# The begin of the MLPs, reordered: fewer parts between the rounds, six products of the second pair in front, modulation one unit on

## Chip, cores and metric

The kernel runs on one core of one Trainium2 chip. The metric is device time in microseconds of one launch. A core has TensorE (PE, matrix products into eight PSUM banks of 128 x 512 fp32), VectorE (DVE), ScalarE (ACT), GpSimd (POOL) and SyncE (SP), which issues nearly all DMAs here. Each engine works through its own instructions in order and waits on semaphores of the others.

## The reference, cut to what matters

Two residual blocks with an MLP each (layers 0 and 1), then a third block with an adaptive modulation. What the change touches:

```python
for l in range(2):
    ...
    mo = memory_attention(mq, mk, mv)                       # layer 0: "m0"
    x = x + jnp.concatenate([mixed, mo], axis=-1) @ w_out[l]
    x = x + jnp.square(jax.nn.relu(rms_norm(x, mlp_norm[l]) @ w_up[l])) @ w_down[l]
...
mod = jax.nn.silu(c) @ w_ada + b_ada                        # 1024 -> 3072, for the third block
```

Sequence 1024, width 1024, MLP width 4096, all fp32.

## The kernel before, in words

**Numbers.** Every fp32 operand of a large product is split into a high part (ACT, a rounding copy to fp32r) and a low part (DVE, the rest), and a product is three matmuls: high x high, high x low, low x high.

**The memory stage of layer 0** (`pe_mem0`, `act_mem0`, `dve_mem0`, `sp_x0`) runs in ten units. PE weaves memory scores, transposes and values with `fill()`: half products of the output projection into bank 7, 24 matmuls each, two a unit in units 0 to 5 and one after. Bank 7 is free again once DVE has added it to X (`dve_x_half`, L1192). DVE does per unit the softmax statistics (L873), the split's low part (L241), the adds, and three of the 24 steps of the modulation sum (`dve_ada`, L1835 for the first three, L1837 after): step j multiplies row block j of `w_ada` by the condition and adds it up. SP loads eight blocks of X and then in every unit three row blocks (waiting for the step that frees the buffer) and one block of projection weights. At the end PE sums the modulation over partitions (L1560).

**The output rest** (`act_out_rest`, `dve_out_rest`): PE makes eight row blocks of the projection (L279), in the order `ROWS = (0, 4, 1, 5, 2, 6, 3, 7)`, DVE adds each to X (L1417), and between these adds DVE and ACT already make the MLP's operands. The normalisation factor is applied after the up product, so the operands are made from X times the norm's weight. The up product is a Strassen-Winograd scheme: X is cut in four quadrants (tokens LOW and HIGH, blocks n < 4 and n >= 4), and from them come seven parts T0 to T6 of four rows k each: T0, T3 and T6 are quadrants (ACT, `act_part`, L1352), T5 and T4 a quadrant less T0 or T6 (DVE, L1371), T2 = T6 - T5 and T1 = T2 - T3 (DVE, L1377). Each row of each part has a high half (ACT, `act_part_hi`, L1357) and a low half (DVE, `dve_part_lo`, L1363). Squares of X go to ACT (L420), their running sum to DVE (`dve_sum`, L427).

**The MLP** goes over 16 pairs j of 256 hidden units. For each pair four weight quarters come by DMA, DVE makes the combinations S1 to S4 of them (`dve_made`, L1270 to L1282), and a ring of three slots holds the weights of the products: `act_ring` (L1255) the high half, `dve_ring` (L1261) the low half, number i = 7j + o for product o of pair j. A product (`pe_product`, L1452) is 12 matmuls. The seven products lie in banks 0, 3, 1, 0, 2, 4, 4; those of one bank add up, and between them their results are taken out: `act_first_sum` (S1 of the results, L1570) frees product 3, `dve_t` of "22" (L1615) frees product 6, "11" (L1607, which needs the root) frees product 0 of the next pair, and so on. Results are scaled with the root (`dve_r`), squared after relu (`dve_q`, L1631), split (`act_up` L1583, `dve_up_lo` L1589), and go into 16 down groups of 6 matmuls (`pe_down`, L1452 also), each of which DVE adds to X (`dve_add`, L1642); down weights are split by `act_down` (L1315) and `dve_down` (L1320).

**The root** at the MLP's begin: PE sums the squares over partitions with a matrix of ones (`pe_total`, L373 and L375, plain fp32), DVE makes the mean (L382), ACT logarithm and exponential (L389, L393), DVE one Newton step (L400 to L407).

The order on every engine is the order in which the code writes it; there is no scheduler. The functions follow.

## Time and profile before

| | us |
|---|---|
| median of 3 runs (3101.41 to 3102.85) | 3102.57 |
| the profiled execution, its own time | 3102.74 |
| its span | 3101.0 |
| PE busy in it | 2969.4 (96%) |
| DVE busy | 2147.3 (69%) |
| ACT busy | 1242.0 (40%) |
| PE matmuls of the MLPs (L1452, 5760) | 1324.9, 31.9 idle before them |
| PE matmuls of the projections (L279, 4560) | 1067.6, 45.6 idle before them |

PE is busy for nearly the whole span, so the time is its work plus its waits. A wait is read in the timeline: each row is a run of like instructions on one engine with its start, its length and, in brackets, how long the engine stood idle before it and what ended that.

### The profile page before, as it was taken

The numbers are of one execution on the slowest core, as the hardware profiler recorded it, in microseconds if no ns is written. First come the engines' busy times: TensorE is split into PE (matmuls) and PEld (weight loads), VectorE is DVE, ScalarE is ACT, GpSimd is POOL, SyncE is SP. The second block draws the span as 40 slices with busy tenths as digits, with TensorE's granted clock in tenths as the row PEclk, the third lists the DMA queues.
The fourth block names the chain that finished last, engine by engine and source line by source line (L and its number), as shares of the span: only waits on it lengthen the run. The fifth ranks groups of instructions, "written<-read, shape, count | busy, mean of one in ns | idle before, by whom it ended". The sixth has DMA issues, their size and how long they took to land.

```text
span 3101.0 us, 35174 instructions
## 1 busy us (share of the span) xinstructions
PE 2969.4 (96%) x13878; PEld 2317.9 (75%) x13888; DVE 2147.3 (69%) x3306; ACT 1242.0 (40%) x2119; POOL 89.8 (3%) x70
## 2 busy tenths in 40 slices
PE   8998979979999999999899899999999999999998
PEld 7885557768888888887777678888888786666666
DVE  7747856677777777688864777777777734666675
ACT  4215642332222222478842522222222515776652
POOL 0003420000000000000000000000000000000000
PEclk9999999999999999999999999999999999999999
DMA  4420024111111111211131011111112131000213
GB/s 152 117 91 8 1 104 135 47 41 55 51 51 48 55 55 55 99 38 51 44 136 35 23 53 54 55 55 51 48 51 68 41 130 34 21 21 21 96 44 120
DMA packets 72804, 190.47 MB, mean 61 GB/s; under 512 B 8320, under 2 KB 8704, under 8 KB 72512
## 3 DMA queue, kind: packets, MB, share of 16 engines
q1 hardware_dynamic: 72640, 188.23, 18.8%
q8 instruction: 110, 1.80, 0.2%
q14 instruction: 54, 0.44, 0.0%
HBM read 172.20 MB, written 14.68 MB: 60 GB/s over the span
## 4 chain that ended last, share of the span: by engine, by line
PE 74%; DVE 13%; ACT 10%; issue 2%; DMA 1%; POOL 0%; SPq 0%; DVEq 0%; ACTq 0%; POOLq 0%
PE PS L1452 42%; PE PS L279 19%; PE PS L334 4%; DVE sm L873 2%; ACT p L891 1%; PE PS L852 1%; DVE p L1995 1%; PE PS L2631 1%; PE PS L2648 1%; PE PS L838 1%; DVE p L241 1%; PE PS L864 1%; PE PS L2622 1%; PE PS L1057 1%; PE PS L1049 1%
## 5 line engine op out<-in xcount | busy, mean ns | idle before, releaser
L1452 PE MATMUL PS<-p 128*128 128x512 f32 x5760 | 1324.9, 392 | 31.9 <-ACT p L1352 16.0
L1452 PEld LDWEIGHTS PS<-p 128*128 128x128 f32 x5760 | 1087.0, 189 | 268.5 <-issue 29.1
L279 PE MATMUL PS<-p 128*128 128x512 f32 (+1 forms) x4560 | 1067.6, 392 | 45.6 <-DVE p L1192 9.7
L279 PEld LDWEIGHTS PS<-p 128*128 128x128 f32 x4560 | 844.4, 190 | 257.9 <-issue 40.7
L1642 DVE TENSOR_TENSOR p<-p,PS 128x512 f32<-128x512 f32 x480 | 328.3, 684 | 70.8 <-PE PS L1452 59.1
L241 DVE TENSOR_TENSOR p<-p 128x1024 fp32r<-128x1024 f32 x138 | 164.0, 1192 | 144.6 <-ACT p L233 144.4
L1261 DVE TENSOR_TENSOR p<-p 128x512 fp32r<-128x512 f32 x224 | 154.4, 689 | 114.0 <-ACT p L1255 112.9
L1583 ACT ACTIVATE p<-p 128x512 fp32r<-128x512 f32 x128 | 80.5, 629 | 372.9 <-DVE p L1631 372.9
L1255 ACT ACTIVATE p<-p 128x512 fp32r<-128x512 f32 x224 | 139.4, 625 | 179.3 <-PE PS L1452 171.7
L233 ACT ACTIVATE p<-p 128x1024 fp32r<-128x1024 f32 x138 | 141.1, 1029 | 164.7 <-PE PS L279 100.1
L891 ACT ACTIVATE p<-PS,sm 128x256 f32<-128x256 f32 (+2 forms) x256 | 127.9, 508 | 188.6 <-DVE sm L877 96.3
L1315 ACT ACTIVATE p<-p 128x512 fp32r<-128x512 f32 x128 | 80.8, 631 | 257.5 <-DMA p<-in_dn_dram 184.9
L334 PE MATMUL PS<-p 128*128 128x512 f32 (+2 forms) x672 | 111.0, 327 | 1.2 <-ACT p L2537 1.2
L873 DVE TENSOR_REDUCE sm<-PS 128x2 f32<-128x768 f32 (+3 forms) x96 | 94.8, 987 | 23.6 <-PE PS L936 12.0
L1320 DVE TENSOR_TENSOR p<-p 128x512 fp32r<-128x512 f32 x128 | 87.9, 687 | 30.7 <-ACT p L1315 30.6
L334 PEld LDWEIGHTS PS<-p 128*128 128x128 f32 x672 | 98.7, 190 | 13.0 <-ACT p L2537 1.6
L852 PE MATMUL PS<-cf,p 128*128 128x128 f32 x600 | 88.3, 281 | 16.1 <-ACT p L917 6.5
L852 PEld LDWEIGHTS PS<-cf,p 128*128 128x128 f32 x600 | 66.3, 142 | 43.4 <-issue 14.0
L1025 POOL TENSOR_SCALAR p<-p,sm 128x384 f32<-128x384 f32 (+1 forms) x64 | 87.7, 1371 | 248.8 <-DVE sm L907 248.8
L1589 DVE TENSOR_TENSOR p<-p 128x512 fp32r<-128x512 f32 x128 | 88.0, 688 | 5.9 <-ACT p L1583 2.8
L1631 DVE SCALAR_TENSOR_TENSOR p<-p 128x512 f32<-128x512 f32 x128 | 87.7, 685 | 0.2
L2746 DVE SCALAR_TENSOR_TENSOR p<-p 128x1024 f32<-128x1024 f32 (+3 forms) x48 | 45.9, 957 | 44.8 <-ACT p L2703 44.8
(230 smaller groups left out, 2696.7 us busy)
## 6 DMA issues: line engine op xcount, KB each, us to landing
p<-in_in_dram SPq DMA_DIRECT2D x72, 512.0 KB, 3.5
p<-in_up_dram SPq DMA_DIRECT2D x128, 256.0 KB, 2.6
p<-in_dn_dram SPq DMA_DIRECT2D x128, 256.0 KB, 2.6
p<-in_out_dram SPq DMA_DIRECT2D x42, 512.0 KB, 3.5
p<-in_ada_dram SPq DMA_DIRECT2D x24, 512.0 KB, 4.3
p<-in_x_dram SPq DMA_DIRECT2D x16, 512.0 KB, 7.9
p<-in_kv_dram SPq DMA_DIRECT2D x16, 512.0 KB, 3.5
spill_dram<-p SPq DMA_DIRECT2D x16, 512.0 KB, 3.6
```

Source lines behind the costliest of these rows:

```text
L233: e.activation(wsp[:, b % NS, 0, 0:n], raw[:, b % NR, 0:n], ACT.Copy).then_inc(*A.did(("whi", b)))
L241: e.tensor_tensor(wsp[:, b % NS, 1, 0:n], raw[:, b % NR, 0:n], fz(wsp[:, b % NS, 0, 0:n]), ALU.subtract).then_inc(*V.did(("wlo", b)))
L279: ins = e.matmul(ps[:, c:c + m], weights(b, j, wi), x[:, c:c + m], start=first and i == 0, stop=end and i == 2)
L334: ins = e.matmul(dst, l[:, t * 128:t * 128 + 128], w[:, wi, :], start=per == 1 and k == 0 and i == 0, stop=k == 7 and i == 2, skip_group_c ...
L852: ins = e.transpose(PS[:, TB[kb], pos * 128:(pos + 1) * 128], Pb[:, u % 2, pos, kb * 128:(kb + 1) * 128], ident)
L873: e.tensor_reduce(mx, S, AX.X, ALU.max).then_inc(*V.did(("mx", tag, hs)))
L891: ins = e.activation(d, S[:, i, :], ACT.Exp, bias=nb[:, i:i + 1], scale=scale, accum_out=sm_[:, i:i + 1])
L1255: e.activation(ring[s3][:, 0, :], quarter[PART[o]][:, :], ACT.Copy).then_inc(*A.did(("ah", l, i)))
L1261: e.tensor_tensor(ring[i % 3][:, 1, :], quarter[PART[o]][:, :], fz(ring[i % 3][:, 0, :]), ALU.subtract).then_inc(*V.did(("al", l, i)))
L1452: ins = e.matmul(PS[:, bank, :], w[:, wi, :], x[:, xi, :], start=start and i == 0, stop=stop and i == 2, skip_group_check=open_)
L1589: e.tensor_tensor(hidden_of(j, hf)[:, 1, k, :], QUOTA[part], fz(hidden_of(j, hf)[:, 0, k, :]), ALU.subtract).then_inc(*V.did(("ul", l, j, ...
L1642: e.tensor_tensor(X[:, r, cs], X[:, r, cs], PS[:, down_bank(l, j, hf, r), :], ALU.add).then_inc(*V.did(("xd", l, j, hf, r)))
```

## The change

1. **Modulation.** In `dve_mem0`, unit u now does steps 3u - 3 to 3u - 1 (units 1 to 8) in place of 3u to 3u + 2 (units 0 to 7). The SP code is as before, and its waits for those steps with it. Step 0 also writes a constant column `eps`.
2. **Output rest.** T4 (its four rows, high and low) and the low parts of T6 leave the rounds; the low part of T5 goes from the round of its n >= 4 to the next round, the low part of T0 from there to the end of the round before. The sum of square 6 is left out; square 6 gets a buffer of its own.
3. **Total.** PE adds square 6 and square 7 itself: six fp32 products in place of four. It stands behind products 0, 1 and 2 whole (before: product 0 and the first three rows of products 1 to 3). The mean is made by ACT (Identity with scale, bias `eps`) in place of DVE, ahead of the root and of ring 5.
4. **First pairs.** PE does products 0 to 5 of pair 1, then all 16 down groups of pair 0, then product 6 of pair 1 (before: products 0 to 2, eight downs, 3 to 5, eight downs, 6). ACT and DVE have a new, written-out order for pairs 0 and 1. First sums of pair 1 get their own buffer. From pair 2 on everything is as before.

Parts 2 to 4 are in both layers, part 1 in layer 0.

```diff
-                if u < 8:
-                    dve_ada(V, e, 3 * u)
+                if 1 <= u <= 8:
+                    dve_ada(V, e, 3 * u - 3)
...
+                    act_part_hi(A, e, l, 3, k)
                     if k < 3:
-                        act_part_hi(A, e, l, 3, k)
-                        act_part_hi(A, e, l, 6, k)
                         act_square(A, e, ("x", l), i, *SQX, X[:, n, :], ready)
                         act_part_hi(A, e, l, 1, k)
                         act_part_hi(A, e, l, 2, k)
-                        act_part_hi(A, e, l, 4, k)
+                        act_part_hi(A, e, l, 6, k)
...
-                        dve_part_lo(V, e, l, 4, k - 1)
+                        dve_part_lo(V, e, l, 5, k - 1)
                         dve_sum(V, e, ("x", l), i - 1, *SQX)
                     block_lo(V, e)
                     dve_part(V, e, l, 5, k)
+                    dve_part_lo(V, e, l, 0, k)
                 else:
-                    dve_part_lo(V, e, l, 0, k)
-                    dve_sum(V, e, ("x", l), i - 1, *SQX)
-                    dve_part(V, e, l, 4, k)
+                    if k < 3:
+                        dve_sum(V, e, ("x", l), i - 1, *SQX)
                     dve_part(V, e, l, 2, k)
                     dve_part(V, e, l, 1, k)
-                    if k < 3:
-                        dve_part_lo(V, e, l, 5, k)
-                        dve_part_lo(V, e, l, 3, k)
-                        dve_part_lo(V, e, l, 6, k)
+                    dve_part_lo(V, e, l, 3, k)
...
-            for o, k1 in ((0, 4), (1, 3), (2, 3), (3, 3)):
-                pe_product(P, e, l, 0, o, 0, k1)
-            pe_total(P, e, ("x", l), SQX[0], SQX[1][1], summed(("x", l)), p=3)
-            for o in (1, 2, 3):
-                pe_product(P, e, l, 0, o, 3, 4)
-            for o in (4, 5, 6):
+            for o in range(3):
                 pe_product(P, e, l, 0, o)
+            pe_total(P, e, ("x", l), SQX[0], SQX[1][7], X_SUMMED[l], p=3, more=SQX[1][6])
+            for o in range(3, 7):
+                pe_product(P, e, l, 0, o)
+
+            for o in range(6):
+                pe_product(P, e, l, 1, o)
+            for hf in range(2):
+                for r in range(8):
+                    pe_down(P, e, l, 0, hf, r)
+            pe_product(P, e, l, 1, 6)
...
+            for k in range(4):
+                dve_part(V, e, l, 4, k)
+            ring(4)
+            for k in range(4):
+                dve_part_lo(V, e, l, 4, k)
+            dve_s2(V, e, l, 0)
+            ring(5)
+            dve_part_lo(V, e, l, 5, 3)
+            for k in range(4):
+                dve_part_lo(V, e, l, 6, k)
+            ring(6)
+            dve_s3(V, e, l, 0)
+            dve_t(V, e, l, 0, "21")
+            ring(7)
+            dve_t(V, e, l, 0, "22")
+            dve_root(V, e, ("x", l), *ROOTX)
+            dve_t(V, e, l, 0, "11")
+            ring(8)
```

DVE in unit 0 of the memory stage before: statistics, first modulation step (L1835), split (L241), the adds (L1192).

```order
L873 TENSOR_REDUCE sm<-PS 128x4 [waits s_pe]
L877 TENSOR_SCALAR sm<-sm 128x4 [waits s_dve]
L1835 TENSOR_SCALAR p<-p,sm 128x1024 [waits s_ada0]
L241 TENSOR_TENSOR p<-p 128x1024 [waits s_act]
L1192 TENSOR_TENSOR p<-p,PS 128x512 [waits s_xl00,s_pe]
L1835 TENSOR_SCALAR p<-p,sm 128x1024 [waits s_ada1]
L1192 TENSOR_TENSOR p<-p,PS 128x512 [waits s_dve,s_pe]
```

The same place of the changed kernel, on to unit 1 (the step is now L1936, the add L1195).

```order
L876 TENSOR_REDUCE sm<-PS 128x4 [waits s_pe]
L880 TENSOR_SCALAR sm<-sm 128x4 [waits s_dve]
L241 TENSOR_TENSOR p<-p 128x1024 [waits s_act]
L1195 TENSOR_TENSOR p<-p,PS 128x512 [waits s_xl00,s_pe]
L1195 TENSOR_TENSOR p<-p,PS 128x512 [waits s_dve,s_pe]
L910 RECIPROCAL sm<-sm 128x4
L914 TENSOR_SCALAR p<-p,sm 128x256 [waits s_dve]
L914 TENSOR_SCALAR p<-p,sm 128x256 x3
L876 TENSOR_REDUCE sm<-PS 128x4 [waits s_pe]
L880 TENSOR_SCALAR sm<-sm 128x4 [waits s_dve]
L1934 MEMSET sm 128x1 [waits s_ada0]
L1936 TENSOR_SCALAR p<-p,sm 128x1024
```

The first step moved behind the next unit's statistics.

ACT before, at the MLP's begin of layer 0, from product 0's first sum (L1570) to the first relu part (L1583); L389 and L393 are the root.

```order
L1570 ACTIVATE p<-PS 128x512 [waits s_pe]
L1255 ACTIVATE p<-p 128x512 [waits s_q12]
L420 ACTIVATE p<-p 128x1024
L1357 ACTIVATE p<-p 128x512 x2
L1255 ACTIVATE p<-p 128x512 [waits s_pe]
L389 ACTIVATE p<-p 128x512 [waits s_dve]
L389 ACTIVATE p<-p 128x512
L393 ACTIVATE p<-p 128x512 [waits s_act] x2
L1255 ACTIVATE p<-p 128x512 [waits s_pe]
L1255 ACTIVATE p<-p 128x512 [waits s_pe,s_dve]
L1583 ACTIVATE p<-p 128x512 [waits s_dve]
```

The same stretch of the changed kernel, without its last row (L1575 first sum, L1261 ring, L1363 high parts, L1659 the mean).

```order
L1575 ACTIVATE p<-PS 128x512 [waits s_pe]
L1261 ACTIVATE p<-p 128x512 [waits s_q12]
L423 ACTIVATE p<-p 128x1024
L1363 ACTIVATE p<-p 128x512
L1261 ACTIVATE p<-p 128x512 [waits s_pe]
L1363 ACTIVATE p<-p 128x512 [waits s_dve] x4
L1659 ACTIVATE p<-PS,sm 128x1024 [waits s_pe]
L391 ACTIVATE p<-p 128x512 [waits s_act]
L391 ACTIVATE p<-p 128x512
L395 ACTIVATE p<-p 128x512 [waits s_act] x2
L1261 ACTIVATE p<-p 128x512
L1261 ACTIVATE p<-p 128x512 [waits s_pe]
```

Ring 4 moved in front of T4's four high parts, and the mean stands between these and the root.

## Rows read from the trace of the kernel before

**Rows 1.** Waits of PE over the span: line, releaser: us, times, longest.

```profile
PE PS L279 <- DVE p L1192: 9.7, 3, 8.1
```

**Rows 2.** Timeline, PE, memory stage: start, length, what, idle before and releaser.

```profile
433.45 6.02 PE L279 MATMUL PS<-p 128*128 128x512 f32 x24
447.54 7.32 PE L279 MATMUL PS<-p 128*128 128x512 f32 x24 [8.07 <-DVE p L1192]
...
463.68 5.74 PE L279 MATMUL PS<-p 128*128 128x512 f32 x24 [0.77 <-DVE p L1192]
```

**Rows 3.** Timeline, DVE, unit 0 of the memory stage.

```profile
445.01 0.75 DVE L1835 TENSOR_SCALAR p<-p,sm 128x1024 f32<-128x1024 f32 x1 [9.53 <-DMA p<-in_ada_dram]
445.68 1.22 DVE L241 TENSOR_TENSOR p<-p 128x1024 fp32r<-128x1024 f32 x1
446.81 0.68 DVE L1192 TENSOR_TENSOR p<-p,PS 128x512 f32<-128x512 f32 x1
```

**Rows 4.** Timeline, ACT, the split's high part in unit 0.

```profile
437.33 1.07 ACT L233 ACTIVATE p<-p 128x1024 fp32r<-128x1024 f32 x1
```

**Rows 5.** First X block's landing, and the page's modulation DMAs (KB, us to landing).

```profile
L1087 SPq DMA_DIRECT2D p<-in_x_dram x1: 327/327/327, 430.4 to 430.4; - x1
DMA to landing us min/median/max: 3.7/3.7/3.7
p<-in_ada_dram SPq DMA_DIRECT2D x24, 512.0 KB, 4.3
```

**Rows 6.** Timeline, PE, begin of the MLP in layer 0.

```profile
631.51 8.86 PE L1452 MATMUL PS<-p 128*128 128x512 f32 x30 [7.99 <-ACT p L1352]
640.21 1.02 PE L373 MATMUL PS<-p,cf 128*128 128x512 f32 x2
641.07 1.02 PE L375 MATMUL PS<-p,cf 128*128 128x512 f32 x2
...
653.53 5.46 PE L1452 MATMUL PS<-p 128*128 128x512 f32 x12 [3.51 <-DVE p L1261]
...
683.92 96.44 PE L1452 MATMUL PS<-p 128*128 128x512 f32 x424 [2.05 <-DVE p L1261]
```

**Rows 7.** Timeline, PE, begin of the MLP in layer 1.

```profile
1766.40 9.66 PE L1452 MATMUL PS<-p 128*128 128x512 f32 x30 [8.00 <-ACT p L1352]
...
1789.21 4.47 PE L1452 MATMUL PS<-p 128*128 128x512 f32 x12 [3.50 <-DVE p L1261]
...
1819.42 140.88 PE L1452 MATMUL PS<-p 128*128 128x512 f32 x613 [2.05 <-DVE p L1261]
```

**Rows 8.** Windows: length, busy and count of PE, PEld, DVE, ACT, POOL, PEclk, DMA, GB/s.

```profile
447.50:451.00 3.50, 3.46 (x8) 2.78 (x9) 0.65 (x1) 0.00 (x0) 0.00 (x0) 0.51 0.85 296
684.00:720.00 36.00, 36.00 (x159) 29.77 (x160) 29.37 (x47) 7.75 (x14) 0.00 (x0) 1.00 0.21 59
```

**Rows 9.** Timeline, DVE, output rest and begin of the MLP in layer 0.

```profile
588.88 1.22 DVE L1417 TENSOR_TENSOR p<-p,PS 128x1024 f32<-128x1024 f32 x1 [2.42 <-PE PS L279]
...
625.94 1.89 DVE L1363 TENSOR_TENSOR p<-p 128x512 fp32r<-128x512 f32 x3
...
630.68 0.69 DVE L1363 TENSOR_TENSOR p<-p 128x512 fp32r<-128x512 f32 x1
...
643.85 1.23 DVE L382 TENSOR_SCALAR p<-PS 128x1024 f32<-128x1024 f32 x1 [5.32 <-PE PS L375]
...
648.59 0.68 DVE L400 TENSOR_TENSOR p<-p 128x512 f32<-128x512 f32 x1
649.31 0.69 DVE L403 SCALAR_TENSOR_TENSOR p<-p 128x512 f32<-128x512 f32 x1
...
652.70 0.69 DVE L1261 TENSOR_TENSOR p<-p 128x512 fp32r<-128x512 f32 x1
```

**Rows 10.** Timeline, ACT, the same stretch: a PSUM copy and two copies in a row.

```profile
636.10 0.58 ACT L1570 ACTIVATE p<-PS 128x512 f32<-128x512 f32 x1
...
647.20 1.14 ACT L1255 ACTIVATE p<-p 128x512 fp32r<-128x512 f32 x2
```

More of the change, by code:

```diff
@@ L373, in pe_total @@
                 ins = e.matmul(ps[:, cs], ones, acc[:, cs], start=True, stop=False)
+                if more is not None:
+                    ins = e.matmul(ps[:, cs], ones, more[:, cs], start=False, stop=False)
                 last = last_sq[c // 512] if isinstance(last_sq, list) else last_sq[:, cs]
@@ L426, in dve_sum @@
                     e.wait_ge(*s)
-                e.tensor_tensor(acc, acc, sqs[k % 2], ALU.add).then_inc(*V.did(("sum", tag, k)))
+                e.tensor_tensor(acc, acc, sqs[k] if isinstance(sqs, dict) else sqs[k % 2], ALU.add).then_inc(*V.did(("sum", tag, k)))
         def summed(tag):
@@ L1215, in program @@
         sa, sb_, sc, sd = (at(188 + 2 * i, [128, 512])[:, :] for i in range(4))
-        SQX = (buf(76), [buf(88), buf(92)])
+        sa1 = at(176, [128, 512])[:, :]
+        SQX = (buf(76), {k: buf((88, 92)[k % 2]) if k != 6 else buf(72) for k in range(1, 8)})
+        X_SUMMED = [[("sum", ("x", l), 5), ("sq", ("x", l), 6), ("sq", ("x", l), 7)] for l in range(2)]
+        eps = sm[:, 120:121]
         ROOTX = (buf(72), buf(32), buf(36), buf(40))
@@ L1517, in pe_mlp @@
                         pe_down(P, e, l, j - 1, 0, r)
-                for o in range(ahead, 6):
+                for o in range(6):
                     pe_product(P, e, l, j, o)
@@ L1567, in act_first_sum, with quota @@
         def act_first_sum(A, e, l, j):
[L1568 removed]
+            for s in A.need(("pp", l, j, 0), ("sum", ("x", l), 4), ("tot", ("x", l)) if j == 1 else None,
+                            ("ul", l, j - 1, "12") if j > 1 else None):
                 e.wait_ge(*s)
[L1570 removed]
+            e.activation(quota(j, "12"), PS[:, 0, :], ACT.Copy).then_inc(*A.did(("s1", l, j)))
         SPOT = {"11": (0, 0), "21": (0, 1), "12": (1, 0), "22": (1, 1)}
         QUOTA = {"11": sd, "21": sc, "12": sa, "22": sb_}
+        def quota(j, part):
+            return sa1 if (j, part) == (1, "12") else QUOTA[part]
         def act_up(A, e, l, j, part):
@@ L1673, in act_mlp, with dve_first_pairs, ring, add @@
                     act_ring(A, e, l, i + 8)
-                    act_down(A, e, l, j, 0)
-                    if j == 0:
-                        act_ring(A, e, l, 9)
-                    act_down(A, e, l, j, 1)
-                    act_down(A, e, l, j, 2)
-            A.cap = (BEHIND[1] if l == 0 else len(ORDER)) - 1
+                    for c in range(3):
+                        act_down(A, e, l, j, c)
+            A.cap = (BEHIND[1] if l == 0 else len(ORDER)) - 1
+        def dve_first_pairs(V, e, l):
+            def ring(*idx):
+                for i in idx:
+                    dve_ring(V, e, l, i)
+            def add(hf, r):
+                dve_add(V, e, l, 0, hf, r)
+            for k in range(4):
[6 more added lines that the diff above has]
+            dve_part_lo(V, e, l, 5, 3)
+            for k in range(4):
+                dve_part_lo(V, e, l, 6, k)
[7 more added lines that the diff above has]
+            ring(8)
+            for name in ("S1", "S3", "S2"):
+                dve_made(V, e, l, 1, name)
+            dve_q(V, e, l, 0, "11")
+            dve_r(V, e, l, 0, "21")
+            ring(9)
+            dve_up_lo(V, e, l, 0, "11")
+            dve_q(V, e, l, 0, "21")
+            dve_r(V, e, l, 0, "22")
+            dve_down(V, e, l, 0, 0)
+            dve_up_lo(V, e, l, 0, "21")
+            dve_q(V, e, l, 0, "22")
+            ring(10)
+            dve_made(V, e, l, 1, "S4")
+            dve_t(V, e, l, 0, "12")
+            dve_down(V, e, l, 0, 1)
+            dve_r(V, e, l, 0, "12")
+            ring(11)
+            dve_q(V, e, l, 0, "12")
+            dve_up_lo(V, e, l, 0, "22")
+            dve_down(V, e, l, 0, 2)
+            ring(12)
+            dve_up_lo(V, e, l, 0, "12")
+            dve_down(V, e, l, 0, 3)
+            dve_s2(V, e, l, 1)
+            ring(13)
+            add(0, 0)
+            dve_t(V, e, l, 1, "11")
+            add(0, 1)
+            dve_s3(V, e, l, 1)
+            add(0, 2)
+            dve_q(V, e, l, 1, "11")
+            add(0, 3)
+            dve_t(V, e, l, 1, "21")
+            add(0, 4)
+            dve_t(V, e, l, 1, "22")
+            add(0, 5)
+            dve_r(V, e, l, 1, "21")
+            add(0, 6)
+            dve_q(V, e, l, 1, "21")
+            add(0, 7)
+            ring(14)
+            add(1, 0)
+            dve_up_lo(V, e, l, 1, "11")
+            add(1, 1)
+            dve_up_lo(V, e, l, 1, "21")
+            add(1, 2)
+            ring(15)
+            add(1, 3)
+            dve_r(V, e, l, 1, "22")
+            add(1, 4)
+            dve_down(V, e, l, 1, 0)
+            add(1, 5)
+            dve_q(V, e, l, 1, "22")
+            add(1, 6)
+            dve_down(V, e, l, 1, 1)
+            add(1, 7)
+            for name in ("S1", "S3", "S2"):
+                dve_made(V, e, l, 2, name)
+            dve_down(V, e, l, 1, 2)
@@ new lines, in dve_mlp @@
+                down = j - 1 if j < 15 else -1
+                dve_down(V, e, l, j - 1, 3)
+                dve_add(V, e, l, down, 0, 0)
+                dve_up_lo(V, e, l, j - 1, "22")
+                dve_add(V, e, l, down, 0, 1)
+                dve_t(V, e, l, j - 1, "12")
+                dve_add(V, e, l, down, 0, 2)
+                dve_ring(V, e, l, i + 2)
+                dve_add(V, e, l, down, 0, 3)
+                dve_r(V, e, l, j - 1, "12")
+                dve_add(V, e, l, down, 0, 4)
@@ L1833, in dve_ada @@
                 e.wait_ge(*s)
+            if j == 0:
+                e.memset(eps, EPS).then_inc(*V.did(("eps",)))
             if k == 0:
```

157 lines of the change are left out of this document (73 added, 84 removed).

## Prediction

> **What bounds the kernel now.** I read the waits of TensorE (PE) first, since it is the busiest engine and whatever it waits for ends the program later. Two of its waits are in this change's reach: one of 8.1 us behind the VectorE (DVE) add L1192 [rows 1], and two of 8.0 us behind the making of the MLP parts, one in each layer [rows 6, 7]. Then I read the PE timeline around both.
>
> In the memory stage PE ends its first half product at 439.47 (433.45 + 6.02), idles 8.07 us, and then needs 7.32 us for the 24 matmuls that take 6.02 us before and 5.74 later [rows 2]. DVE shows why: the first modulation sum starts at 445.01, after 9.53 us of waiting for a DMA, and behind it stand the split and the add that frees PE's bank [rows 3]. Nothing else was late: the split's other half ended on ScalarE (ACT) at 438.40 [rows 4], and the add's X block landed 3.7 us after its issue at 430.4, at 434.1 [rows 5].
>
> At the MLP's begin PE waits 7.99, later 3.51 and 2.05 us, and the stretches after the long waits run slow [rows 6]; layer 1 does the same 1134.89 us later [rows 7]. Undisturbed, 424 matmuls take 96.44 us, 0.2275 each: 2.73 a product, 1.365 a down group. The granted clock is 0.51 after the 8.07 wait (the 1.2 GHz level most of that stretch) and 1.00 later (2.4 GHz) [rows 8].
>
> **The change, term A: modulation one unit on.** In unit 0 nothing now stands between DVE's statistics and its split. The split starts at 438.43; the add follows 1.13 behind (445.68 to 446.81 today [rows 3]), waits for PE's 439.47, and runs from 439.57 to 440.25. PE resumes at 440.29 instead of 447.54: 7.25. Its idle is then 0.8, after which I expect the full clock, as after 0.77 at 463.68 [rows 2]: 5.74 instead of 7.32: 1.6. In unit 1 the modulation sum that stood ahead of the normalisation (pitch 0.67) is gone, so most of the 0.77 wait at 463.68 goes: 0.67. Sum 9.5 us, once. From here to the out projection PE has no large wait, and there DVE starts from a wait for PE (588.88 [rows 9]), so all of it shifts.
>
> What moves: each unit keeps three sums; 21 of the 24 modulation DMAs on SP wait a unit longer, and the out0 loads, queued behind them on SP, are issued at a unit's end rather than in its middle. A load feeds a split three units on, and a unit is some 15 us (447.54 to 463.68 [rows 2]): nothing. A modulation DMA lands 4.3 us after its issue [rows 5], and its sum is due a unit later: nothing. The last sum comes behind unit 8's add; before PE's modulation products stands one more half product, 24 x 0.2275 = 5.5 us: nothing. The memset of `eps` is one short operation: nothing.
>
> **Term B: the begin of the MLPs.** I set up the DVE, ACT and PE queues of layer 0 in their new order, on today's times, as if A were not there. Prices [rows 9, 10]: DVE 512 wide 0.60 from start to start (0.69 long), 0.72 if it needs the one before (648.59 to 649.31); 1024 wide 1.13; ACT 512 wide 0.53, PSUM copy 0.5; 0.03 between DVE and ACT, 0.14 into PE (652.70 + 0.69 to 653.53).
>
> *Up to the first product.* Part 4 and the low parts of 4 and 6 leave the rounds, low part 0 moves in front of the next X add, the sum of square 6 goes. An odd round lasts 6.95: the X add, 1.22, then ACT's two parts, high part, square, three high parts and ring, 5.0, and the ring's low part, 0.6; DVE waits about 2 us in it, so a lighter DVE gains nothing there. An even round is X add, three low parts, sum, T5 (about 0.7) and low part 0, 5.44, the first with a projection split, 1.13, more; round 3 has S1, S3, S2 behind it, 2.17. From 588.88 this gives X adds at 595.83, 602.38, 611.50, 616.94, 623.88 and 629.32. Low part 0, row 3, ends 629.41 instead of 631.37 (630.68 + 0.69), and PE resumes at 629.55 instead of 631.51: 1.96 sooner.
>
> *The sums of squares.* T1's last row ends 634.12, so product 1's last row starts 634.26; the slow clock's loss (30 matmuls in 8.86 rather than 6.8) mostly hides in that wait. Products 0 to 2 end 637.67. The total is six matmuls of 0.86 [rows 6], 1.72 more: to 642.83. The mean goes to ACT; no row has it. Bounds: the 512 wide PSUM copy, 0.58, doubled, 1.16; DVE's own 1.23. I take 1.1, near the first, since it is the same engine and source. The Trainium skill (ScalarE: Activation LUTs, "Rules for kernel authors") would have adds and multiplies on VectorE, not ScalarE, and so speaks against this move; on DVE the operation takes 1.23 [rows 9], and the sum by that rule would be 0.1 a layer more, not less, so the rows do not bear the rule out here. The same page ("What ACT_TABLE_LOAD costs") puts an ACTIVATE with a pointer bias at about 280 ns + 0.833 ns an element, an estimate of 1.13 us for this one, with the same sum; no run here shows it yet.
>
> *Chain behind the total.* The mean ends 644.12, the root's ACT part takes 2.12 as today (645.08 to 647.20 [rows 9, 10]), ring 5 ends 646.87; DVE idles from 642.7 for it, since ring 5 is queued behind the root. Ring 5's low half from 646.90, five low parts, ring 6, S3, T21, ring 7, T22 are nine steps of 0.60 and one of 0.72: T22 ends 653.71. PE has products 3 to 5 done at 651.02 and waits 2.8 for T22. Root (six DVE operations, four of them waiting for the one before, 4.2) and T11: to 658.52; PE is through product 6 at 656.58 and waits 2.1. Then DVE does ring 8, three S and the square of 11 (to 661.88), ACT up 11 and ring 9, DVE ring 9 and the square of 21 (664.97), ACT up 21 and down 0, DVE down 0 and the square of 22 (668.08), ACT up 22, down 1, first sum and ring 10 (670.28), DVE ring 10: to 671.00; PE has pair 1's products 0 to 2 done at 666.85 and waits 4.3. So product 3 of pair 1 starts at 671.14 whatever PE does before. From there 144 matmuls (three products, 16 down groups, product 6) remain: 32.76, to 703.9, with rings 11 and 12 in time within 0.4.
>
> Today 168 of the same 264 matmuls (two pairs of 84, 96 of downs) stand before 683.92, so they end at 683.92 + 96 x 0.2275 = 705.76, in layer 1 at 1819.42 + 21.84 = 1841.26, or 706.37 on layer 0's time [rows 6, 7]. So the edit is worth 1.5 to 2 us per layer if the clock holds. It probably does not: after today's 3.51 us waits a product took 5.46 and 4.47 us instead of 2.9 [rows 6, 7], 2.6 and 1.6 lost, and after 2.05 us (683.92) nothing. A wait of 4.3 is nearer the first; I take their mean, 2.1. A slow stretch behind the shorter waits would cost nothing, since product 3 of pair 1 waits for DVE and ACT in any case. Layer 0 then ends at 706.0 (+0.2), layer 1, whose slow stretch at the first product is longer by up to 0.75, at 706.4 (0).
>
> **Sum.** Profiled execution 3102.74 (span 3101.0), less 9.5, plus 0.2: 3093.4; the median of the runs lies 0.17 below that execution, so **3093.3 us**.
>
> **Rivals.** *The MLP begin gains too.* If the clock holds behind the 4.3 wait, and mean and high parts come a little sooner than my ledger has them, each layer gains 1.5 to 4, 3 to 8 in all: about 3088. For it: every link is priced with a full hand-over. Against it: rows 6 and 7 after 3.51 us.
>
> *A comes to little or is handed back.* If the later sums or loads hold PE in a following unit, the gain would be lost to a wait of the same kind: 3102 at worst. Against it: the first sum's DMA was late (445.01 [rows 3]) only because eight X blocks stand ahead of it on the queue; later ones take 4.3 us and have a unit's time. The same result comes if each MLP's chain is 4 to 5 us longer than worked out: 3098 to 3102.
>
> *Slower.* The mechanism is the chain total, mean, root, ring 5, ..., ring 10 on ACT and DVE, which fixes product 3 of pair 1. It is 28.2 us in my ledger (642.83 to 671.0) against 19.1 us of PE work (seven products). Each microsecond more is one per layer; from 4.7 us more (32.9) the kernel is no faster than now, from 7.8 more it is slower by the 0.2% (6.2 us) that a measurement of this kernel can tell from no change. About 40 hand-overs at 0.12 us more each would reach the first mark: 3103 to 3110.
>
> **How the numbers follow.** Forecast 0.58; MLP gains 0.20; handed back 0.16; slower 0.06. The forecast's own spread is about 2 us a layer, so 3089 to 3097; bound for faster by 0.2% is 3096.4. Faster: nearly all of the first two, 0.77. Same: the third and a little of the first and last, 0.19. Slower 0.04. To hold 8 in 10 the range takes most of the second and the near part of the third: 3086 to 3099.
>
> **What would show it.** A: PE's wait at 447.54 is about 1 us and the following 24 matmuls take under 6; the first modulation sum stands behind unit 1's statistics without a wait. B: PE's first wait in the MLP 6 us instead of 8; waits of about 2.8, 2.1 and 4.3 us before product 6, pair 1's products 0 and 3; 144 matmuls behind the last of them. It would be wrong if the 8 us wait reappears behind another DMA, or if DVE has no idle stretch before ring 5.

## Result and profile after

The changed kernel takes 3083.78 us (median of four runs, 3082.28 to 3091.04), the kernel before in the same comparison 3101.99; the ratio is 0.9945, with a 95% interval of 0.9933 to 0.9957. The gain is 18.2 us where 9.3 were forecast, and the time lies 2.2 us below the forecast's range. Five more runs, told below, gave 3084.50 to 3092.83; all nine have the median 3085.01 and the mean 3086.6. One run of all that are told here, of another kernel, had a granted clock of 0.749 over its whole length and took 3702.0 us; medians and ranges are those of the others.

The two traces say where it came from. First what the edit touches. These are TensorE's (PE's) waits in the kernel after, with the us in total, the number and the longest; they answer [rows 1]:

```profile
PE PS L1455 <- DVE p L1369: 12.7, 2, 6.3
...
PE PS L1455 <- DVE p L1267: 8.3, 2, 4.1
...
PE PS L1455 <- DVE p L1624: 5.4, 2, 2.7
```

The wait behind the add of the half product, 9.7 us in all before, is 1.7 now. The MLP's 8.0 is 6.3, and 2.7 and 4.1 are new. The PE timeline of the memory stage after, to be held against [rows 2] (start, us, line, shapes, count, and in brackets the idle time before it and what ended it):

```profile
427.82 1.97 PE L1052 MATMUL PS<-p 128*128 128x256 f32 x8 [1.52 <-DVE p L1015]
429.43 5.84 PE L279 MATMUL PS<-p 128*128 128x512 f32 x24
436.07 5.74 PE L279 MATMUL PS<-p 128*128 128x512 f32 x24 [0.80 <-DVE p L1195]
...
449.96 5.71 PE L279 MATMUL PS<-p 128*128 128x512 f32 x24
```

The wait fell from 8.07 to 0.80, the 24 matmuls behind it from 7.32 to 5.74, and the wait of 0.77 at the end of the unit is gone. But note the first two rows: the row ahead of the first half product took 3.65 us before and takes 1.97 now, and the half product itself starts 4.02 us sooner, ahead of anything that the edit moves. The row before, and the next of its kind, which takes 1.89 us:

```profile
430.36 3.65 PE L1049 MATMUL PS<-p 128*128 128x256 f32 x8 [1.51 <-DVE p L1012]
...
454.70 1.89 PE L1049 MATMUL PS<-p 128*128 128x256 f32 x8
```

Of the 4.02 us, 2.8 are busy time of PE (403.4 us up to there before, 400.6 after) and 1.2 are shorter waits.

The begin of the MLP in layer 0, against [rows 6]:

```profile
604.34 2.20 PE L1455 MATMUL PS<-p 128*128 128x512 f32 x9
612.88 8.40 PE L1455 MATMUL PS<-p 128*128 128x512 f32 x27 [6.34 <-DVE p L1369]
621.11 1.02 PE L373 MATMUL PS<-p,cf 128*128 128x512 f32 x2
...
637.33 4.57 PE L1455 MATMUL PS<-p 128*128 128x512 f32 x12 [2.69 <-DVE p L1624]
642.16 8.44 PE L1455 MATMUL PS<-p 128*128 128x512 f32 x36 [0.26 <-DVE p L1616]
654.75 45.53 PE L1455 MATMUL PS<-p 128*128 128x512 f32 x193 [4.15 <-DVE p L1267]
```

The waits of 6.34, 2.69 and 4.15 us stand where the forecast had 6, 2.8 and 4.3. Layer 1 repeats them (6.34, 2.70, 0.25, 4.15). The chain in between, first ScalarE's (ACT) timeline after, from the mean to ring 5 (compare [rows 10]):

```profile
626.46 1.12 ACT L1659 ACTIVATE p<-PS,sm 128x1024 f32<-128x1024 f32 x1 [3.44 <-PE PS L377]
...
629.71 1.14 ACT L1261 ACTIVATE p<-p 128x512 fp32r<-128x512 f32 x2
```

and VectorE's (DVE), from the low half of ring 5 to T22 (compare [rows 9]):

```profile
630.36 0.69 DVE L1267 TENSOR_TENSOR p<-p 128x512 fp32r<-128x512 f32 x1 [4.39 <-ACT p L1261]
...
636.50 0.68 DVE L1624 TENSOR_TENSOR p<-p,PS 128x512 f32<-128x512 f32 x1
```

The mean takes 1.12 us, and DVE idles 4.39 us until ACT has come past mean and root to ring 5.

**The ledger.** Seven places of the program have a PE row that can be found in both traces: the first half product (433.45 before), the end of unit 0 (463.68), the start of the first and the end of the last row of the MLP of layer 0 (621.32, 1299.05) and of layer 1 (1756.20, 2446.94), and the end of the last row of all (3088.70). How much sooner or later the kernel after is there, taken as steps from place to place in us (minus is sooner):

| stretch ending at | forecast | after |
|---|---|---|
| first half product | 0 | -4.02 |
| end of unit 0 | -9.5 | -9.70 |
| first row of MLP 0 | 0 | -3.26 |
| last row of MLP 0 | +0.2 | +0.26 |
| first row of MLP 1 | 0 | +1.26 |
| last row of MLP 1 | 0 | -3.30 |
| last row | 0 | -1.71 |
| all | -9.3 | -20.47 |

Term A hit, and so did term B in layer 0. What was missed is in the stretches that the forecast had at 0: term B in layer 1, and four stretches that are in no term. The total here is that of one profiled run each (3082.28 against 3102.74), hence 20.5 and not 18.2.

### The profile page after: what moved, and what is told of

The parts are those of the page before. It is cut to its first block, busy times and chain, and to the rows that moved or that the text cites. A ratio compares the mean times of both kernels' runs of the same rounds, so it can differ in the third digit from the quotient of the medians.

```text
span 3080.5 us, 35195 instructions
## 1 busy us (share of the span) xinstructions
PE 2964.4 (96%) x13896; PEld 2313.5 (75%) x13896; DVE 2143.6 (70%) x3303; ACT 1243.7 (40%) x2121; POOL 89.7 (3%) x70
## 4 chain that ended last, share of the span: by engine, by line
PE 74%; DVE 13%; ACT 11%; issue 2%; POOL 0%; DMA 0%; DVEq 0%; SPq 0%; ACTq 0%; POOLq 0%
PE PS L1455 41%; PE PS L279 20%; PE PS L334 4%; DVE sm L876 2%; ACT p L894 1%; PE PS L855 1%; DVE p L2096 1%; PE PS L2732 1%; PE PS L2749 1%; PE PS L841 1%; PE PS L867 1%; DVE p L241 1%; PE PS L2723 1%; PE PS L1060 1%; DVE p L1369 1%
## 5 line engine op out<-in xcount | busy, mean ns | idle before, releaser
L241 DVE TENSOR_TENSOR p<-p 128x1024 fp32r<-128x1024 f32 x138 | 163.9, 1191 | 147.3 <-ACT p L233 147.1
L1261 ACT ACTIVATE p<-p 128x512 fp32r<-128x512 f32 x224 | 139.6, 625 | 169.9 <-PE PS L1455 160.8
```

Of the source, the lines that this page charges most:

```text
L241: e.tensor_tensor(wsp[:, b % NS, 1, 0:n], raw[:, b % NR, 0:n], fz(wsp[:, b % NS, 0, 0:n]), ALU.subtract).then_inc(*V.did(("wlo", b)))
L1261: e.activation(ring[s3][:, 0, :], quarter[PART[o]][:, :], ACT.Copy).then_inc(*A.did(("ah", l, i)))
```

## Experiments

**The two parts alone.** First the modulation alone, in the kernel before:

```diff
-                if u < 8:
-                    dve_ada(V, e, 3 * u)
+                if 1 <= u <= 8:
+                    dve_ada(V, e, 3 * u - 3)
...
```

> Only the modulation steps move one unit on; the MLPs are those of before. Theory 1 (the waits are as forecast, and what the changed kernel gained beyond them, some 9 us, is TensorE's clock falling or not falling in stretches that the edit does not touch): the wait of 8.1 us at the second half product falls to 0.8, the first 24 matmuls behind it take 5.7 instead of 7.3 us, together 9.7 us; the total is 3102 - 9.7 = 3092, and may lie up to 5 us to either side by slow stretches elsewhere, which the granted clock by windows then shows. Theory 2 (the MLP edit itself brought the other 8 to 9 us): 3092 within 1 us.

Measured: 3090.97 us (five runs, 3087.56 to 3094.78), ratio 0.9963 (0.9950 to 0.9975): 10.9 us gained. Its PE timeline has the edit's part as the changed kernel has it, and the MLP as the kernel before:

```profile
430.24 3.65 PE L1049 MATMUL PS<-p 128*128 128x256 f32 x8 [1.51 <-DVE p L1012]
433.37 5.99 PE L279 MATMUL PS<-p 128*128 128x512 f32 x24
440.18 5.74 PE L279 MATMUL PS<-p 128*128 128x512 f32 x24 [0.82 <-DVE p L1192]
...
618.68 9.96 PE L1452 MATMUL PS<-p 128*128 128x512 f32 x30 [8.00 <-ACT p L1352]
```

The step to the end of unit 0 is -9.53. The rows ahead of it are those of the kernel before: 3.65 us, and no 4 us gained.

Then the rest alone, the changed kernel with the modulation steps back in their old places:

```diff
-                if 1 <= u <= 8:
-                    dve_ada(V, e, 3 * u - 3)
+                if u < 8:
+                    dve_ada(V, e, 3 * u)
...
```

> Only the MLP edit; the modulation steps stand where they stood before (step 0 still writes eps). Theory 1: from the first product to the begin of pair 2 each layer takes what it took before within 1 us (the shorter first wait is paid back by the waits before product 6 and before product 3 of pair 1, 2.7 and 4.2 us), so 3102, up to 5 us to either side by slow stretches elsewhere. Theory 2: 3093.5, with each layer's MLP begin 4 us shorter.

Measured: 3102.72 us (eleven runs, 3095.31 to 3105.15), ratio 0.9998 (0.9989 to 1.0007). By the median the new begin of the MLPs alone is worth nothing that can be measured, as the forecast had it. The runs fall in two groups, four at 3095.31 to 3098.30 with a granted clock of 0.987 and seven at 3102.68 to 3105.15 with 0.985 or 0.986, and the trace is of the fastest of the eleven, 7.4 us under their median:

```profile
427.63 1.97 PE L1052 MATMUL PS<-p 128*128 128x256 f32 x8 [1.51 <-DVE p L1015]
429.25 5.83 PE L279 MATMUL PS<-p 128*128 128x512 f32 x24
444.58 7.82 PE L279 MATMUL PS<-p 128*128 128x512 f32 x24 [9.49 <-DVE p L1195]
...
667.73 32.59 PE L1455 MATMUL PS<-p 128*128 128x512 f32 x136 [4.15 <-DVE p L1267]
```

Here the half product is 4.2 us sooner than before, as in the changed kernel, and the wait for the modulation's data is longer for it (9.49 in place of 8.07): of the 4.2 us 2.5 are left at the end of the unit. Where a wait for data stands next, time won ahead of it is partly lost there.

By the medians the two parts add to -10.1 us (-10.9 + 0.8), the whole gave -18.2, or -15.3 by the mean of its nine runs. So 5 to 8 us come from neither part by itself.

**Does the moment of the start matter?** All five engines carry the same instructions in the same order, line numbers aside, up to the first modulation sum at about 435 us, so the first 4 us of the ledger cannot be the order of instructions. One way in which a moved program could meet another clock is the time that has passed since the launch. The kernel before was started later, by three memsets on DVE that the first DMA waits for:

```diff
+            for s in S.need(("late", 2)):
+                e.wait_ge(*s)
...
+            for i in range(3):
+                for s in V.need(("late", i - 1) if i else None):
+                    e.wait_ge(*s)
+                e.memset(buf(92), 0.0).then_inc(*V.did(("late", i)))
```

> The kernel before, with three memsets of a 128 x 1024 tile on VectorE ahead of the first DMA, so that the whole program starts about 2 us later and is otherwise the same. Theory 1: every wait of TensorE is as before, but the stretches at the low granted clock fall on other places, and the total minus the delay differs from before by several us (1.5 to 8). Theory 2: the total is that of before plus the delay, within 1 us, with the same slow stretches.

Measured: 3104.64 us (eleven runs, 3102.80 to 3106.38). Its first DMA is issued at 4.32 us in place of 0.72; less these 3.60 us (about 2 had been expected) the kernel takes 3101.0, within 1 us of its time without them: the change of several us that theory 1 expected did not come. The slow stretches moved, though: the half product is 0.20 us sooner than in the kernel before in spite of the 3.60 us delay, and 2.14 us are given back up to the end of the unit, where the wait for the modulation's data is 9.7 us in place of 8.1.

The changed kernel was run again as it is, with one memset and with three:

> The changed kernel itself, to have its time from as many runs as the experiment with the MLP edit alone has. Theory 1 (the edit is worth the forecast's 9.3 us, and what it gained beyond that is clock that comes and goes between runs): the median of many runs lies near 3091 us, between the sum of the two parts run alone (10.9 gained, 0.8 lost, so 3102 - 10.1 = 3092) and the 3083.8 of the first four runs, with single runs from 3082 to 3094. Theory 2 (the edit itself sets how the clock falls in the stretches around it, so its gain is a fixed 18 us): median within 2 us of 3084, all runs within 3 us of it.

> The changed kernel with one memset of VectorE ahead of its first transfer (the whole program starts about 1.2 us later, nothing else is moved). Theory 1 (the clock comes and goes between runs whatever the start): time less the delay is that of the changed kernel in the same call, within 1 us. Theory 3 (the moment at which a sparse stretch comes, counted from the launch, decides whether the clock falls in it): time less the delay differs from the changed kernel's by several us in either direction, since the stretches at 85 to 100, 420 to 433 and 555 to 590 us fall in other cases. Theory 2: within 1 us of the changed kernel, which stays at 3084.

> The changed kernel with three memsets of VectorE ahead of its first transfer (3.6 us later, as the kernel before had it in an earlier run, which was back at its own time less the delay). Theory 1: time less 3.6 us is the changed kernel's in the same call, within 1 us. Theory 3: several us beside it, in either direction, and beside the run with one memset.

Measured: as it is 3087.22 us (five runs, 3084.50 to 3092.83; ratio 0.9955, 0.9943 to 0.9968); with one memset 3090.85 (five runs), 3089.6 less its delay of 1.22 (first DMA at 1.94 us); with three 3093.02 (seven runs), 3089.4 less 3.60. The fixed gain of 18 us is refuted by the first of these: single runs of one and the same kernel lie up to 10.5 us apart (3082.28 to 3092.83 over all nine). Theory 1's median of 3091 was not met either, only its range of single runs. The nine stand in the order of their granted clock: 0.990 in the two runs up to 3082.56 us, 0.989 in the three up to 3085.01, 0.988 in 3087.22 and 3089.50, 0.987 in 3091.04, 0.986 in 3092.83. The kernel before has 0.986 or 0.987 in all its 21 runs. Whether the later start costs the 2.2 to 2.4 us that stand between these medians stays open, since the ratios' intervals overlap (0.9943 to 0.9968 as it is, 0.9955 to 0.9980 with one memset).

**The ledger of every kernel.** Now the steps of the table above for the traces of all these, each against the same trace of the kernel before, in us. The first column contains the delay of the start where there is one:

| kernel | half product | end of unit 0 | MLP 0 first | MLP 0 last | MLP 1 first | MLP 1 last | end | all |
|---|---|---|---|---|---|---|---|---|
| changed | -4.02 | -9.70 | -3.26 | +0.26 | +1.26 | -3.30 | -1.71 | -20.47 |
| changed, again | -3.64 | -9.70 | -3.24 | +0.25 | +1.33 | -3.25 | 0.00 | -18.25 |
| changed, one memset | -1.71 | -9.69 | -1.59 | +0.22 | +1.30 | -3.52 | +2.74 | -12.25 |
| changed, three memsets | -0.18 | -9.68 | -3.19 | +0.37 | +1.32 | -3.49 | +2.79 | -12.06 |
| modulation alone | -0.08 | -9.53 | -3.23 | +2.65 | -0.10 | +0.16 | -1.66 | -11.79 |
| MLP begins alone | -4.20 | +1.73 | -1.57 | +0.31 | +1.24 | -3.33 | -1.66 | -7.48 |
| before, three memsets | -0.20 | +2.14 | -1.64 | -0.12 | +2.11 | +0.34 | +0.01 | +2.64 |

Column by column: the modulation is worth 9.53 to 9.70 us in each of the five traces that have it. The MLP of layer 0 is 0.22 to 0.37 us longer in each of the five that have the new begin. The kernels without it give 0, -0.12 and, in the modulation alone, +2.65: the old begin itself is not the same from trace to trace, which is taken up under term B below. The steps at the half product, at the first row of MLP 0 and at the end go with no edit: about -4 at the half product stands in the MLP begins alone and not in the modulation alone, and, less the delay of 3.60, -3.8 in the kernel before that merely started later; -3.2 at the first row of MLP 0 stands in the modulation alone, and -1.6 there in the delayed kernel before. At the first row of MLP 0 they come in pieces of 1.6 us. The clearest column besides that goes with an edit is the MLP of layer 1: -3.25 to -3.52 in the five traces with the new begin, +0.34 or less in the three without. The stretch ahead of it, +1.24 to +1.33 in those five, has +2.11 in the delayed kernel before too and is not assigned.

**Loosening the chain.** If the chain from the total to ring 10 sets product 3 of pair 1, a shorter chain must show its whole worth. In the changed kernel ring 5 goes ahead of the mean on ACT, the root is split in two halves of which T11 needs one, and the first sum of pair 1 with ring 10 goes right behind ring 9 (rings 11 and 12 move up with it):

```diff
             act_ring(A, e, l, 9)
+            act_first_sum(A, e, l, 1)
+            act_ring(A, e, l, 10)
...
             dve_r(V, e, l, 0, "21")
             ring(9)
+            ring(10)
```

> The changed kernel with the chain behind the total loosened: ring 5 ahead of the mean on ScalarE; on VectorE the root's low half ahead of ring 6, T11 behind T22 and the root's high half behind that; the first sum of pair 1 and ring 10 right behind ring 9 on both engines. Theory 1: the chain of VectorE and ScalarE fixes the start of product 3 of pair 1; loosened, TensorE's waits of 2.7 and 4.2 us fall to 1 and 0, no slow stretch follows, and each layer ends its begin 7 to 9 us sooner: 3083.8 - 16 = 3068. Rival (TensorE's waits there are set by something else, such as the quarters' DMAs): under 4 us in all, 3080 to 3084.

Measured: 3074.81 us (four runs, 3069.82 to 3079.50), ratio 0.9912 (0.9898 to 0.9925). In layer 0 these are the waits left behind the first one:

```profile
638.24 16.61 PE L1458 MATMUL PS<-p 128*128 128x512 f32 x72 [0.87 <-DVE p L1627]
656.50 3.69 PE L1458 MATMUL PS<-p 128*128 128x512 f32 x15 [1.65 <-DVE p L1269]
```

2.69 + 0.26 + 4.15 became 0.87 + 1.65, 4.6 us a layer or 9.2 in all. Only the order and the waits on DVE and ACT were changed, so their chain was the bound. That the time fell by 9.0 us from the first 3083.78 looks like the same number, but is chance: against the trace of the changed kernel the steps of the two MLPs are 7.87 us (-7.61 after +0.26) and 6.62 us (-9.92 after -3.30) shorter, 14.5 in all, and the other five give 5.4 back. Beyond the 9.2 us of waits the MLPs thus gained 5.3, mostly slow rows that no longer came. Against the 16 us expected, 3.3 stand in the new wait for ring 12, which is late next. It was put sooner, two steps on ACT and six on DVE (not three on both, as the expectation says):

```diff
             act_down(A, e, l, 0, 0)
+            act_ring(A, e, l, 12)
             act_up(A, e, l, 0, "22")
             act_down(A, e, l, 0, 1)
-            act_ring(A, e, l, 12)
...
             dve_down(V, e, l, 0, 0)
+            ring(12)
```

> The changed kernel with the loosened chain of the earlier run, and ring 12 of the weights split three steps sooner on both engines. In that run (3074.8 us) TensorE still waited 1.65 us ahead of product 5 of pair 1 for ring 12 in layer 0, and 1.66 us in layer 1. If the begin of the MLP is bound by the chain on VectorE and ScalarE, as the ledger of the prediction has it, both waits go and the time is 3.3 us less, 3071.5 us; if VectorE as a whole is the bound, ring 12 only moves the wait to the next product (down 0 of pair 0, whose low part is then 0.6 us later) and the time stays at 3074.8 us.

Measured: 3066.69 us (four runs, 3064.27 to 3071.66), ratio 0.9889 (0.9876 to 0.9903). The wait for ring 12 is gone in both layers:

```profile
640.20 40.18 PE L1458 MATMUL PS<-p 128*128 128x512 f32 x176 [0.87 <-DVE p L1627]
```

Over MLP 0 this is 1.54 us, as expected (step -9.15 after -7.61); over MLP 1 it is 3.45 (-13.37 after -9.92), since a slow stretch at that MLP's end is gone as well. The 8.1 us between the medians are more than the two waits hold, and do not repeat: run a second time, the same kernel took 3070.33 us (median of 3067.01, 3070.33 and 3071.93). This kernel, some 33 us under the kernel before, is the fastest of the study.

> The kernel with the loosened chain and the earlier ring 12 itself, for the comparison with the filled one on the same chip: 3066.7 us as before, single runs from 3064 to 3072.

**One kernel, two traces.** These two runs of an identical program show by themselves what the unexplained steps are. They were taken on two chips, which by itself need not be the reason: on one chip, five runs of the changed kernel had granted clocks from 0.986 to 0.989. PE rows ahead of the first half product and at the modulation products, first run:

```profile
425.50 1.08 PE L869 MATMUL PS<-p 128*64 128x256 f32 x8
...
430.36 1.97 PE L1054 MATMUL PS<-p 128*128 128x256 f32 x8 [1.51 <-DVE p L1017]
...
556.46 6.13 PE L1567 MATMUL PS<-cf,p 128*128 128x1 f32 x48
```

And the same two places on PE's timeline in the second run:

```profile
424.56 1.98 PE L869 MATMUL PS<-p 128*64 128x256 f32 x8
...
430.44 3.53 PE L1054 MATMUL PS<-p 128*128 128x256 f32 x8 [1.51 <-DVE p L1017]
...
558.13 8.17 PE L1567 MATMUL PS<-cf,p 128*128 128x1 f32 x48
```

Eight matmuls took 1.08 us in one run and 1.98 in the other, the eight ahead of the half product 1.97 and 3.53, the modulation's 48 took 6.13 and 8.17. The granted clock of the stretch from 420 to 436 us, in the table by stretches, was 1.00 in the first run (columns: stretch, length, busy us of PE, its weight loads, DVE, ACT, POOL, then the granted clock, DMA share, GB/s)

```profile
420.00:436.00 16.00, 12.04 (x71) 7.99 (x69) 7.70 (x23) 6.77 (x24) 3.25 (x3) 1.00 0.29 103
```

and 0.79 in the second:

```profile
420.00:436.00 16.00, 12.24 (x54) 7.73 (x55) 6.65 (x18) 4.45 (x16) 3.09 (x3) 0.79 0.29 100
```

In the steps of the ledger the first run has -1.47 at the half product and -1.60 up to MLP 0, the second -0.04 and +0.04; the other steps agree within 0.3 us. So the clock after a sparse stretch may fall to its lower level in one run and not in the next. The Trainium skill says the same (TensorE: Matmul & The Clock Gate, Part 1): the clock's moments of decision do not begin with the kernel, and how many slow matmuls a kernel has differs from run to run. By that rule a later start is no remedy, and the kernel before with its memsets, within 1 us of its time less the delay, agrees; the two traces above agree with the second half, with about 1.6 us for each fall.

**Filling the waits.** If the clock falls because PE stood, work that nobody reads should keep it up, and save the slow rows behind a wait. In the changed kernel and in the one with ring 12 sooner, products into a free bank were put into the waits:

```diff
+        def pe_warm(P, e, n):
+            for s in P.need(P.held[5]):
+                e.wait_ge(*s)
+            for _ in range(n):
+                half_product(e, 5, TS[0, 0][:, :, 0:128], TS[0, 0], True, True, False)
...
             for k in range(k0, k1):
+                if (j, o, k) == (0, 0, 3):
+                    pe_warm(P, e, 8)
```

> The changed kernel with products that nobody reads (two operands that are already there, into bank 5, which is free) in three of TensorE's waits in each MLP's begin: 24 matmuls in the 6.34 us ahead of the last quarter of product 0, 9 in the 2.69 us ahead of product 6, 15 in the 4.15 us ahead of product 3 of pair 1. Nothing else is moved. Theory A (TensorE's clock falls because the engine stood, and the price of a wait is the wait plus the slow rows behind it): the granted clock of the begin stays at 1.0, the 27 rows behind the first wait take 6.0 us in place of 8.40, so the sum and the chain to ring 10 come 2.4 us sooner in layer 0 and 2.7 in layer 1, and the rows behind the third wait save 1.7 us more in each; 8 us in all, some 3079 us against 3087.2 for the changed kernel in the last runs. Theory B (the clock falls by its own moments, whatever TensorE does there): the clock in these stretches falls as before and the time is the same or some us longer, since the filling itself then runs at half speed and delays the rows behind it.

> The kernel with the loosened chain and the earlier ring 12 (3066.7 us), with the 24 matmuls in the first wait of each MLP alone, the only long one that it has left there. Theory A: the rows behind that wait take 6.0 us in place of 8.84 and 8.45, 5.3 us in all, 3061.5 us. Theory B: the same or longer.

Measured: 3087.52 us for the changed kernel with three waits filled (five runs, 3081.73 to 3093.35), the same as without; 3068.64 us with the first wait filled where ring 12 is sooner (four runs, 3064.32 to 3074.68), against 3070.33 without. Neither theory holds as it stood. The clock did stay up in layer 0, from 0.84 to 1.00 over the 21.7 us from the MLP's first row (in layer 1 only partly; in the kernel with ring 12 sooner it was 1.00 in both layers). The table by stretches, first of the changed kernel:

```profile
604.30:626.00 21.70, 15.36 (x50) 10.31 (x49) 18.54 (x27) 13.74 (x23) 0.00 (x0) 0.84 0.08 24
```

and of the one with the waits filled:

```profile
609.30:631.00 21.70, 19.04 (x74) 13.31 (x73) 18.56 (x27) 13.82 (x23) 0.00 (x0) 1.00 0.08 24
```

But no time came of it. The filled kernel's PE timeline:

```profile
609.34 2.20 PE L1455 MATMUL PS<-p 128*128 128x512 f32 x9
613.42 8.46 PE L1455 MATMUL PS<-p 128*128 128x512 f32 x36 [1.88 <-DVE p L1423]
622.66 3.66 PE L1455 MATMUL PS<-p 128*128 128x512 f32 x15 [0.78 <-DVE p L1369]
626.16 1.02 PE L373 MATMUL PS<-p,cf 128*128 128x512 f32 x2
```

The sum of squares starts 16.82 us behind the MLP's first row; without the filling, with 27 slow rows of 8.40 us, it is 16.77 (621.11 - 604.34). The bank came free 1.88 us into the wait, so the filling ended about 0.9 us late, and at full speed the rows then wait 0.78 us for the low part of product 1, which the slow rows had met without a wait. All that is left in the trace of 8 us expected is 1.1 us in MLP 0 (step -0.88 in place of +0.25) and 0.8 in MLP 1 (-4.05 in place of -3.25), and the changed kernel's medians show nothing of it. Here 2.4 us of slow rows beside a chain on other engines had cost next to nothing.

## Why the forecast missed

**What bounds the kernel; term A.** Right. 7.25 us of wait, 1.6 of slow matmuls and 0.67 of the next unit were forecast, 9.5 in all; the traces have 9.53 to 9.70. Nothing was late in the units after, and the products of the modulation did not wait.

**Term B, layer 0.** Right in the chain, and in the sum with some luck (below). Moved by the 16.98 us that the MLP begins sooner, the forecast's moments stand beside the trace so: first product 612.57, measured 612.88; total 620.69, measured 621.11; ring 5's low half 629.92, measured 630.36; product 3 of pair 1 654.16, measured 654.75. The mean on ACT, for which no row stood ahead, took 1.12 us, with 1.1 taken. The Trainium skill's figure for it (ScalarE: Activation LUTs, "What ACT_TABLE_LOAD costs"), an estimate of 1.13 us, agrees. Pair 1's first product waited 0.26 us where 2.1 were forecast, because product 6 ahead of it ran slow (12 matmuls in 4.57 us); as the forecast had said, that costs nothing. The loosened chain, which took 9.2 us of waits away by moving work on DVE and ACT alone, shows that the chain was the bound. The luck is in what the sum was set against, MLP 0 of the one trace of before: with the modulation alone the same old begin took 2.65 us more there, and against that trace the new begin gains 2.4 us in layer 0.

**Term B, layer 1.** The step "after 2.05 us (683.92) nothing" failed. For layer 1 it was wrong in the very trace that it was read from. It was read on layer 0, where the clock behind that wait is 1.00 [rows 8]; in layer 1 of the same trace the wait of 2.05 us at 1819.42 [rows 7] is followed by

```profile
1820.00:1830.00 10.00, 10.00 (x39) 8.04 (x39) 6.99 (x12) 1.90 (x3) 0.00 (x0) 0.84 0.35 107
```

that is, by a clock of 0.84 in the next 10 us (the table by stretches again), 1.6 us lost. The same stretch with the modulation alone, behind the wait of 2.05 us at 671.99 in layer 0, is slow too, so what was read on layer 0 did not hold for layer 0 either:

```profile
672.00:682.00 10.00, 10.00 (x37) 8.11 (x38) 6.99 (x12) 2.05 (x4) 0.00 (x0) 0.83 0.34 107
```

The new begin has no such wait there. About as much lies at the end of that MLP, where nothing was changed. PE's timeline before:

```profile
2427.01 1.87 PE L2251 MATMUL PS<-p,cf 128*128 128x512 f32 x2 [2.65 <-ACT p L2316]
2427.89 4.65 PE L1452 MATMUL PS<-p 128*128 128x512 f32 x12
2432.38 1.02 PE L2251 MATMUL PS<-p,cf 128*128 128x512 f32 x2
```

and after:

```profile
2409.89 1.12 PE L2352 MATMUL PS<-p,cf 128*128 128x512 f32 x2 [2.65 <-ACT p L2417]
2410.45 3.32 PE L1455 MATMUL PS<-p 128*128 128x512 f32 x12
2413.61 1.02 PE L2352 MATMUL PS<-p,cf 128*128 128x512 f32 x2
```

The same wait of 2.65 us, and behind it 5.37 us to the next such row in one trace and 3.72 in the other: 1.65 us of slow rows. Together the two falls come to 3.3 us, the step of MLP 1. The three traces with the old begin have this last fall, and of those with the new begin the one with the loosened chain has it too (1.69 us for the first two matmuls), so it does not go strictly with the edit.

**Sum and range.** Here is the step that decided the miss. The sum set the profiled execution of before less the two terms, and so took every other stretch of that one execution as given. They were not: 4.02 + 3.26 + 1.71 us sooner and 1.26 later, and 3.30 in MLP 1, together 11 us. Added up over stretches of 10 us, (1 - granted clock) x PE's busy time is 28.3 us in the profile before, 19.7 in the one after, 23.4 with the modulation alone: some 7 of the 11 us are clock (28.3 less 19.7, less term A's 1.6). The forecast's spread, "about 2 us a layer", had no term for that, though the trace of before shows such stretches far from the edit (3.65 us at 430.36 for eight matmuls that take 1.89 at 454.70). With a term for two falls of 1.6 us more or fewer, the range would have begun at 3082.8 and held the time; that is said with hindsight.

**The rivals.** "The MLP begin gains too" came nearest in time, for other reasons: of its mechanism, the clock holding behind the 4.3 us wait, nothing was seen (0.84 in the 10 us behind the 4.15 us). Handing back and slower did not come.

**What stays open.** The nine runs of the changed kernel average 15.3 us under the kernel before's 3101.9; the terms that go with the edit in every trace are 9.6, less 0.3, and 1.6 to 3.3 in layer 1, 11 to 13 us, and some 2.4 more where the old begin is as slow in layer 0 as with the modulation alone. The two parts alone gave 10.1, the two delayed starts 12.3 to 12.5 with the delay taken off. So 10 to 13 us are the edit's by these runs, and 2 to 5 are not assigned: they may be the luck of nine runs, or an order of work that makes a fall at other places less likely. The granted clock says that much of the 15.3 is clock: 0.9884 on average over the nine runs against 0.9862 over the 21 of before, 0.0022 of 3085 us, an estimate of 6.8 us, too high by what falls into waits. Term A's 1.6 and the 3.3 of layer 1 are in it. Why the kernel before keeps within 4.4 us (3099.42 to 3103.84 in 21 runs) and the changed one scatters over 10.5 was not found either.

## What to carry to other kernels

A forecast made from one profiled execution holds that execution's clock with it: list the stretches where the granted clock is below 1 before pricing an edit, and give the range a term for falls that come and go, also far from the edit. Price what an edit does by the steps between rows that both traces share; here the step of the modulation is 9.42 to 9.70 us in all ten traces that have it, while whole runs of one kernel differ by 10. A step repeats only as far as the clock does: that of MLP 0 with the old begin was 0 in one trace and 2.65 us in another. And when a chain of two helper engines sets a product, put the link that the bound engine needs next ahead of work that is due later: a few moved lines took twice 4.6 us of waits away here.

## What the hardware showed

- The granted clock after a sparse stretch is not a property of the program: the same kernel had 1.00 and 0.79 at 420 to 436 us in two runs, and a fall cost about 1.6 us each time. Over whole runs this is 3064.27 to 3071.93 us for one kernel and 3082.28 to 3092.83 for another, the latter in the order of the runs' granted clock (0.990 down to 0.986).
- A higher granted clock need not be a shorter time: with the waits filled the mean clock of the profiled run rose from 0.989 to 0.992 and the median time stayed (3087.22 and 3087.52 us): the rows behind the first wait then waited 0.78 us for a low part, and the sum of squares began as late as before (16.82 and 16.77 us behind the MLP's first row).
- Time won ahead of a wait for a transfer is partly lost in it: 4.20 us sooner at the half product left 2.47 at the end of the unit.
